# Final norm of an encoder block: three row tiles go through GpSimd and ScalarE, with a root group of their own

## The chip, the cores and the metric

The kernel runs on one NeuronCore of a Trainium2 chip. A core has TensorE (PE), VectorE (DVE), ScalarE (ACT), GpSimd (POOL) and SyncE (SP, which here issues DMAs), an on-chip memory of 128 partitions (SBUF), an accumulator memory that TensorE writes (PSUM), and DMA engines. The metric is the device time of one execution in microseconds, as a median of runs.

## The reference

One block: a mixer of convolutions and projections, a mixture of experts whose output is added to the rows, and a root-mean-square norm of every row at the end. The change touches only what follows the experts:

```
def rmsnorm(x, g):
    y = xf * lax.rsqrt(jnp.mean(xf * xf, axis=-1, keepdims=True) + RMS_EPS)
    return (y * g.astype(jnp.float32)).astype(x.dtype)
...
        x = x + gt2 * hier_moe(h, ...)
    return rmsnorm(x, g_final)
```

There are 1024 rows of 1024 float32 values. `hier_moe` adds, for each row, the outputs of two experts, each scaled by a weight.

## The kernel before

Most of the time is a loop over blocks of 128 (row, expert) pairs: SyncE streams expert weights into SBUF, ScalarE and VectorE split them into a high and a low part, TensorE multiplies, VectorE scales a block's result and GpSimd adds it to the rows `d_x1` in DRAM by an indirect DMA (a scatter). The change lies behind this loop, in the last 40 us.

The rows there are in 8 tiles of 128 rows (tile i is rows 128i to 128i+127, one row on each partition). The rows of the last two expert blocks are handled apart: their results don't go through DRAM, and their rows are called z rows here (`z_x_prev`, `z_x_last`, 128 rows each). Each engine runs its own program in its written order, and semaphores tie them:

- SyncE loads `g_final`, spread over all partitions, into `g_fin`, then the 8 tiles into `f_x` (line 583). Then it waits for tile 0, 1, ... 7 of the output in this order, and stores each (line 586).
- ScalarE takes the sum of squares of each tile and of the two z blocks (`square`, line 1032), and roots of groups of them (`group_root`, line 1041). Groups are ranges of a small table, one column for each of 10 blocks: (0, 2), (2, 5), (5, 10), where columns 8 and 9 are the z blocks.
- VectorE turns sums into mean squares (`mean_square`, line 1632, `f_ms`), and roots into reciprocal roots with a Newton step (`rstd_of`, four short instructions, lines 1638 to 1641). `tile_out` (by `scaled`, line 1645) makes one output tile as `f_x` times `f_rstd` times `g_fin`, in one instruction with two tensors in SBUF. Between them it adds the results of the experts to the z rows: line 1657 for `z_x_prev` (two tensors in SBUF), `y_last` (line 1570: one tensor in PSUM, one in SBUF), and line 1665 for `z_x_last` (PSUM and SBUF). Its last two instructions scale the z rows (`z_o`).
- GpSimd gathers the z rows (line 748), and has nothing to compute after that. At the end it waits until all 8 stores have landed (`f_st`, 16 for each), since a z row overwrites the same row of a stored tile, and then scatters the two z blocks into the output (line 756).

The end of VectorE's program:

```
            tile_out(2, 1)
            tile_out(3, 1)
            dve.wait_ge(y_ev, n_before + 1 + CREDIT_Y)
            dve.wait_ge(s_shared, 1)
            v.tensor_tensor(z_x[1][:], ps[:, 0, :], y_last[:], ALU.add).then_inc(s_z, 1)
            tile_out(4, 1)
            mean_square(2, NT + 2)
            rstd_of(2)
            for i in range(5, NT):
                tile_out(i, 2)
```

Of the kernel before, what the change touches and what calls it, by code (L numbers as in the profile page):

```python
# [29 lines left out]
ALU = mybir.AluOpType  # L30
ACT = mybir.ActivationFunctionType
# [41 lines left out]
def encoder_block(nc, x, c, w_ada, b_ada, g_norm1, w_in, conv_a, w_a_out, conv_b, b_conv_b, ln_g, ln_b,  # L73
                  w_b_out, w_o, g_norm2, w_rg, b_rg, w_re, b_re, w_gate, w_up, w_down, g_final, out):
    S, D = x.shape
    KT = D // P
    NT = S // P
# [13 lines left out]
    with ExitStack() as ctx:  # L91
# [3 lines left out]
        def at(name, offset, shape, dtype):  # L95
            return nc.alloc_sbuf_tensor_at(name, shape, dtype, offset=base + offset)
# [86 lines left out]
        def rt(name, shape, dtype=F32):  # L183
# [65 lines left out]
        f_x = at("f_x", 0, [P, NT, D], F32)  # L249
        y_prev = at("y_prev", (NCH + 4) * 4 * C8, [P, D], F32)  # L250
        y_last = at("y_last", (NCH + 4) * 4 * C8 + T4, [P, D], F32)
        z_x = [at("z_x_prev", oR + GT1 * T4, [P, D], F32), at("z_x_last", oR + A2 * T4, [P, D], F32)]
        f_junk = at("f_junk", (NCH + 2) * 4 * C8, [P, 2, D], F32)
        z_o = at("z_o", (NCH + 3) * 4 * C8, [P, 2, D], F32)
        f_o = [at(f"f_o{i}", o, [P, D], F32) for i, o in enumerate(
            (oX + 4 * T4, oX + 5 * T4, oX + 6 * T4, oX + T4, *((2 * NCH + 2) * 4 * C8 + i * T4 for i in range(4))))]
        g_fin = at("g_fin", oR + SH2 * T4, [P, D], F32)
# [6 lines left out]
        NF = NT + 2  # L264
        f_ss, f_ms, f_root, f_rstd, f_new = (at(n, oM + 2816 + 64 * i, [P, NF], F32)
                                             for i, n in enumerate(("f_ss", "f_ms", "f_root", "f_rstd", "f_new")))
# [16 lines left out]
        def sem(name):  # L283
            return ctx.enter_context(nc.semaphore(name))

        s_par, s_const, s_fill = sem("params_in"), sem("const_ready"), sem("const_steps")
        s_rows_in, s_g2_in, s_wr_in = sem("bias_rows_in"), sem("gfin_in"), sem("router_in")
# [10 lines left out]
        s_ssq, s_rstd, s_xn, s_xT, s_xTev = sem("ssq"), sem("rstd_x"), sem("xn_ready"), sem("xT_ps"), sem("xnT_ready")  # L298
# [5 lines left out]
        s_ln, s_lsig, s_sw, s_bhi, s_blo = sem("ln_t"), sem("ln_sig"), sem("swish"), sem("conf_hi"), sem("conf_lo")  # L304
# [14 lines left out]
        gu_hi, gu_lo, gu_used = sem("gu_hi"), sem("gu_lo"), sem("gu_used")  # L319
# [7 lines left out]
            sem("last_tokens"), sem("same_token"), sem("shared_rows_ps"),  # L327
            sem("z_x_full"))
        s_z, z_out, z_st = sem("z_added"), sem("z_out"), sem("z_stored")
        f_ssq, f_out, f_st = sem("f_ssq"), sem("f_out"), sem("f_stored")  # L330
        a_free, g_free, y_free = sem("short_free"), [sem("gate_a_free"), sem("gate_b_free")], sem("y_free")
        after_wait = sem("after_wait")
        x_full = [sem(f"rows_full{i}") for i in range(NT)]
# [6 lines left out]

        XT_BY_ACT = (3, 5, 6, 7)
        XT_BY_DVE = tuple(i for i in range(NT) if i not in XT_BY_ACT)
        GROUPS = ((0, 2), (2, 5), (5, 10))

        DVE_AT = {}

# [82 lines left out]
        def _(sp):  # L429
# [58 lines left out]
            def load_slab(n):  # L488
                slot, _, before = slab_turn(n)
                sp.wait_ge(w_lo_done, before + 1 + CREDIT_SLAB)  # L490
                sp.dma_start(raw3[:, slot], slab_out(n)).then_inc(wr_full[slot], 16)
# [89 lines left out]
            sp.wait_ge(moe_done, 1)  # L581
            for i in range(NT):
                sp.dma_start(f_x[:, i, :], d_x1[i * P:(i + 1) * P, :]).then_inc(x_full[i], 16)
            for i in range(NT):
                sp.wait_ge(f_out, i + 1)
                sp.dma_start(out[i * P:(i + 1) * P, :], f_o[i][:]).then_inc(f_st, 16)
            sp.wait_ge(f_st, 16 * NT)
            sp.wait_ge(z_st, 32)
# [3 lines left out]
        def _(pool):  # L592
            g = nc.gpsimd
# [122 lines left out]
            n_before = pool.value_load(tab[0:1, NBLK + 1:NBLK + 2], min_val=PAIRS // P - 1, max_val=NBLK - 2)  # L716
# [30 lines left out]
            for n in range(2):  # L747
                g.indirect_dma_start(z_x[n][:], None, d_x1, bass.IndirectOffsetOnAxis(ap=l_idx[:, n:n + 1], axis=0),
                                     bounds_check=S - 1, oob_is_err=False).then_inc(zx_full, 16)


            pool.wait_ge(f_st, 16 * NT)
            pool.wait_ge(s_same, 2)
# [7 lines left out]
        def _(act):  # L761
            a = nc.scalar
# [10 lines left out]
            def square_x(i):  # L773
                act.wait_ge(x_full[i], 16)
                if i >= 2:
                    act.wait_ge(s_ssq, i - 1)
                a.activation(junk0[:, i % 2, :], xn[:, i, :], ACT.Square, accum_out=ss[:, i:i + 1]).then_inc(s_ssq, 1)
# [208 lines left out]
            n_before = act.value_load(tab[0:1, NBLK + 1:NBLK + 2], min_val=PAIRS // P - 1, max_val=NBLK - 2)  # L986
# [41 lines left out]
            def square(n, source):  # L1028

                if n >= 2:  # L1030
                    act.wait_ge(f_ssq, n - 1)
                a.activation(f_junk[:, n % 2, :], source, ACT.Square, accum_out=f_ss[:, n:n + 1]).then_inc(f_ssq, 1)
# [5 lines left out]
            def group_root(p):  # L1038
                gr = slice(*GROUPS[p])
                act.wait_ge(s_msq, 2 * NT + p + 1)  # L1040
                a.activation(f_root[:, gr], f_ms[:, gr], ACT.Sqrt).then_inc(s_root, 1)
# [5 lines left out]
            for i in range(2, 6):  # L1047
                square_x(i)
            group_root(1)
            square_x(6)  # L1050
            square_x(7)
            for n in range(2):
                act.wait_ge(s_z, n + 1)
                square(NT + n, z_x[n][:])
            group_root(2)


        @block.vector
        def _(dve):
# [3 lines left out]
            def step(ins):  # L1063

                steps[0] += 1
                ins.then_inc(dv, 1)
                dve.wait_ge(dv, steps[0])

            def held(s, value):

                dve.wait_ge(s, value)
                dve.sem_inc(after_wait, 1)
# [374 lines left out]
            for i in range(NT):  # L1447
# [23 lines left out]
                scaled = v.scalar_tensor_tensor(hh, xt, rstd[:, i:i + 1], rows[:, A2, :], ALU.mult, ALU.mult)  # L1471
# [45 lines left out]
            for k, first, end in ROW_PARTS:  # L1517
                n = end - first
# [48 lines left out]
            def y_out(dst, blk, used, bank=3):  # L1567

                dve.wait_ge(d_used, used)
                v.scalar_tensor_tensor(dst, ps[:, bank, :], w_all[:, bass.ds(blk, 1)], rows[:, GT2, :], ALU.mult, ALU.mult).then_inc(y_ev, 1)  # L1570
# [10 lines left out]
            n_before = dve.value_load(tab[0:1, NBLK + 1:NBLK + 2], min_val=PAIRS // P - 1, max_val=NBLK - 2)  # L1581
# [47 lines left out]
            def mean_square(p, squares):  # L1629
                gr = slice(*GROUPS[p])  # L1630
                dve.wait_ge(f_ssq, squares)
                v.tensor_scalar(f_ms[:, gr], f_ss[:, gr], 1.0 / D, RMS_EPS, ALU.mult, ALU.add).then_inc(s_msq, 1)

            def rstd_of(p):
                gr = slice(*GROUPS[p])
                dve.wait_ge(s_msq, 2 * NT + p + 1)
                dve.wait_ge(s_root, 2 * NT + p + 1)
                step(v.reciprocal(f_rstd[:, gr], f_root[:, gr]))
                step(v.tensor_tensor(f_new[:, gr], f_rstd[:, gr], f_ms[:, gr], ALU.mult))
                step(v.scalar_tensor_tensor(f_new[:, gr], f_new[:, gr], -0.5, f_rstd[:, gr], ALU.mult, ALU.mult))  # L1640
                v.scalar_tensor_tensor(f_rstd[:, gr], f_new[:, gr], 1.5, f_rstd[:, gr], ALU.add, ALU.mult).then_inc(s_rstd, 1)

            def scaled(dst, source, n, p, done):
                dve.wait_ge(s_rstd, NT + p + 1)
                v.scalar_tensor_tensor(dst, source, f_rstd[:, n:n + 1], g_fin[:], ALU.mult, ALU.mult).then_inc(done, 1)  # L1645

            def tile_out(i, p):
                scaled(f_o[i][:], f_x[:, i, :], i, p, f_out)
# [9 lines left out]
            mean_square(1, 5)  # L1658
            rstd_of(1)
            y_out(y_last[:], n_before, n_before * 2 + 2, 1)  # L1660
            tile_out(2, 1)
            tile_out(3, 1)
            dve.wait_ge(y_ev, n_before + 1 + CREDIT_Y)
            dve.wait_ge(s_shared, 1)
            v.tensor_tensor(z_x[1][:], ps[:, 0, :], y_last[:], ALU.add).then_inc(s_z, 1)
            tile_out(4, 1)
            mean_square(2, NT + 2)
            rstd_of(2)
            for i in range(5, NT):
                tile_out(i, 2)  # L1670
            for n in range(2):
                scaled(z_o[:, n, :], z_x[n][:], NT + n, 2, z_out)


        @block.tensor
        def _(pe):
# [163 lines left out]
            for j in range(KT):  # L1840
                slot, _, _ = slab_turn(n0 + j)
                pe.wait_ge(w_lo_done, n0 + j + 1 + CREDIT_SLAB)
                if j == 1:
                    pe.wait_ge(act_evac, CREDIT_ACT_EVAC + 4 * KT - 1)
                if j >= 2:
                    pe.wait_ge(s_ma, j - 1)
                slab_product(slot, ps[:, j % 2, :], s_alo if j == 0 else None, None,
                             {2: (0, mean_last), 3: (5, variance)}.get(j)).then_inc(pe_slab, 1)
                if j == 1:
                    mean()  # L1850
# [283 lines left out]
```

## Time and profile before

| | |
|---|---|
| median of 3 runs | 1602.11 us (1601.93 to 1602.23) |
| the profiled execution, its own time | 1603.24 us |
| span of its trace, first to last instruction | 1601.6 us |
| PE, DVE, ACT, POOL busy, share of the span | 97%, 83%, 43%, 19% |

The busy shares are means over the whole span and are set by the expert loop. Behind it TensorE has little to do: in the last 20 us it has no instruction. What the end is worth is read from the chain of work that ended last and from the engines' instructions in order of time from about 1562 us on. Times are microseconds from the start of the span; a row of a timeline has the start, the length, the engine, the line, the operation, what is written and read, and its shape.

### The profile page before, as it was taken

How to read it: one execution, taken by the hardware profiler on the slowest of the kernel's cores; microseconds unless marked ns; L12 is line 12 of the kernel's file. 1: busy time of each engine (PE TensorE's matmuls, PEld its weight loads, DVE VectorE, ACT ScalarE, POOL GpSimd, SP SyncE). 2: the span in 40 equal slices, each digit the busy share in tenths (PEclk: the TensorE clock that was granted, in tenths of full speed). 3: DMA queues.
4: the chain of work that ended last, by engine and by line, in shares of the span. 5: the costliest groups of instructions: out<-in, count | busy, mean ns of one | idle time of the engine just before them, and what ended most of it. 6: DMA issues, size and time to landing. Idle time of an engine off the chain costs nothing.

```text
span 1601.6 us, 21226 instructions
## 1 busy us (share of the span) xinstructions
PE 1561.0 (97%) x7106; PEld 1276.8 (80%) x7106; DVE 1325.9 (83%) x1131; ACT 687.2 (43%) x582; POOL 304.8 (19%) x225
## 2 busy tenths in 40 slices
PE   8999999999999999999999999999999999999994
PEld 4788888888888888768888887788888888888882
DVE  5696979797878778789447468999999999999996
ACT  6501111111101010436222126777777777777763
POOL 2000000000101010000001003354344334433441
PEclk9999999999999999999999999999999999999997
DMA  9242333232324141644453347999999999999976
GB/s 359 93 119 79 107 102 108 76 118 65 118 65 129 54 144 46 217 150 140 158 181 138 118 176 271 385 373 398 390 366 369 383 377 389 374 390 385 378 275 239
DMA packets 167951, 352.61 MB, mean 220 GB/s; under 512 B 17479, under 2 KB 91239, under 8 KB 167907
## 3 DMA queue, kind: packets, MB, share of 16 engines
q1 hardware_dynamic: 150836, 309.57, 53.0%
q0 software_dynamic: 16992, 42.32, 8.7%
q8 instruction: 25, 0.41, 0.1%
q10 hardware_dynamic: 81, 0.17, 0.0%
q14 instruction: 17, 0.14, 0.0%
HBM read 324.90 MB, written 46.67 MB: 232 GB/s over the span
## 4 chain that ended last, share of the span: by engine, by line
PE 88%; DVE 6%; DMA 3%; issue 2%; ACT 1%; SPq 0%; DVEq 0%; POOLq 0%; POOL 0%; ACTq 0%
PE ps L1681 28%; PE ps L1683 28%; PE ps L1682 28%; PE ps L2008 2%; DMA xn<-in_x_dram 1%; DVE conv_acc_b L1253 1%; PE ps L2013 1%; DMA w_raw<-in_w_in_dram 1%; DVE e_lo L1545 1%; PE ps L1902 1%; DMA stream<-d_short 1%; DVE f_o L1645 0%; DVE e_lo L1549 0%; PE ps L1886 0%; DMA e_raw<-in_w_down_dram 0%
## 5 line engine op out<-in xcount | busy, mean ns | idle before, releaser
L1681 PE MATMUL ps<-A_hi,w_hi 128*128 128x512 f32 x1024 | 399.8, 390 | 6.0 <-DVE w_lo L1092 4.1
L1683 PE MATMUL ps<-A_hi,w_lo 128*128 128x512 f32 x1024 | 398.6, 389 | 0.0
L1682 PE MATMUL ps<-A_lo,w_hi 128*128 128x512 f32 x1024 | 398.5, 389 | 0.0
L1545 DVE TENSOR_TENSOR e_lo<-e_raw,e_hi 128x2048 fp32r<-128x2048 f32 x132 | 301.1, 2289 | 10.4 <-ACT e_hi L958 10.3
L1253 DVE SCALAR_TENSOR_TENSOR conv_acc_b<-glu,colc,conv_acc_b 128x1024 f32<-128x1024 f32 x232 | 298.0, 1285 | 10.2 <-DVE rows L1238 0.6
L958 ACT CAST e_hi<-e_raw 128x2048 fp32r<-128x2048 f32 x132 | 252.2, 1913 | 44.0 <-PE ps L1683 43.8
L1681 PEld LDWEIGHTS ps<-A_hi,w_hi 128*128 128x128 f32 x1024 | 192.3, 188 | 49.3 <-DVE w_lo L1092 5.4
L1682 PEld LDWEIGHTS ps<-A_lo,w_hi 128*128 128x128 f32 x1024 | 192.2, 188 | 40.2 <-issue 0.5
L1683 PEld LDWEIGHTS ps<-A_hi,w_lo 128*128 128x128 f32 x1024 | 192.2, 188 | 40.0
L1681 PE MATMUL ps<-e_hi,xT_hi 128*128 128x512 f32 x528 | 212.5, 403 | 1.7 <-DVE xT_lo L1553 1.7
L1683 PE MATMUL ps<-e_hi,xT_lo 128*128 128x512 f32 x528 | 207.1, 392 | 0.0
L1682 PE MATMUL ps<-e_lo,xT_hi 128*128 128x512 f32 x528 | 206.4, 391 | 0.0
L1549 DVE TENSOR_TENSOR e_lo<-e_raw,e_hi 128x2048 fp32r<-128x2048 f32 x64 | 146.0, 2283 | 0.0
L697 POOL DMA_INDIRECT d_x<-y_sb,s_idx x31 | 85.9, 2772 | 305.3 <-DVE y_sb L1570 276.7
L812 ACT CAST w_hi<-w_raw 128x1024 fp32r<-128x1024 f32 x72 | 73.6, 1047 | 156.1 <-PE ps L1683 153.1
L964 ACT CAST e_hi<-e_raw 128x2048 fp32r<-128x2048 f32 x64 | 122.3, 1913 | 42.1 <-PE ps L1683 42.1
L1092 DVE TENSOR_TENSOR w_lo<-w_raw,w_hi 128x1024 fp32r<-128x1024 f32 x72 | 88.0, 1223 | 61.0 <-ACT w_hi L812 57.8
L1683 PEld LDWEIGHTS ps<-e_hi,xT_lo 128*128 128x128 f32 x528 | 99.5, 188 | 21.7
L1681 PEld LDWEIGHTS ps<-e_hi,xT_hi 128*128 128x128 f32 x528 | 99.9, 189 | 20.5 <-DVE xT_lo L1553 1.8
L1682 PEld LDWEIGHTS ps<-e_lo,xT_hi 128*128 128x128 f32 x528 | 99.9, 189 | 18.9
L1681 PE MATMUL ps<-e_hi,hT_hi 128*128 128x512 f32 x264 | 104.7, 397 | 3.0 <-DVE hT_lo L1564 3.0
L1683 PE MATMUL ps<-e_hi,hT_lo 128*128 128x512 f32 x264 | 104.2, 395 | 0.0
(329 smaller groups left out, 2001.1 us busy)
## 6 DMA issues: line engine op xcount, KB each, us to landing
e_raw<-in_w_gate_dram SPq DMA_DIRECT2D x132, 512.0 KB
e_raw<-in_w_up_dram SPq DMA_DIRECT2D x132, 512.0 KB
e_raw<-in_w_down_dram SPq DMA_DIRECT2D x66, 1024.0 KB, 7.8
w_raw<-in_w_in_dram SPq DMA_DIRECT2D x56, 512.0 KB, 4.3
stream<-in_w_ada_dram SPq DMA_DIRECT2D x36, 512.0 KB, 5.8
xn<-in_x_dram SPq DMA_DIRECT2D x8, 512.0 KB, 11.3
ada_a<-in_w_ada_dram SPq DMA_DIRECT2D x8, 512.0 KB, 10.4
d_short<-conv_acc_a POOLq DMA_DIRECT2D x8, 512.0 KB, 4.1
```

The costliest lines, as they stand in the source:

```text
L697: g.indirect_dma_start(d_x1, bass.IndirectOffsetOnAxis(ap=idx_ap, axis=0), rows_ap, None, bounds_check=S - 1, oob_is_err=False, compute_op ...
L812: a.copy(w_hi[:, slot, :], w_raw[:, slot, :]).then_inc(w_hi_done, 1)
L958: a.copy(e_hi[:, q, :], e_raw[:, q, :]).then_inc(gu_hi, 1)
L964: a.copy(e_hi[:, 4 + q, :], e_raw[:, 4 + q, :]).then_inc(d_hi, 1)
L1092: v.tensor_tensor(w_lo[:, slot, :], w_raw[:, slot, :], w_hi[:, slot, :].bitcast(F32), ALU.subtract).then_inc(w_lo_done, 1)
L1253: lstep(v.scalar_tensor_tensor(conv_acc_b[:], glu[:, t:t + S], w, conv_acc_b[:], ALU.mult, ALU.add))
L1545: v.tensor_tensor(e_lo[:, q, :], e_raw[:, q, :], e_hi[:, q, :].bitcast(F32), ALU.subtract).then_inc(gu_lo, 1)
L1549: v.tensor_tensor(e_lo[:, 4 + q, :], e_raw[:, 4 + q, :], e_hi[:, 4 + q, :].bitcast(F32), ALU.subtract).then_inc(d_lo, 1)
L1681: t.matmul(dst, st_hi, mv_hi, start=first, stop=False)
L1682: t.matmul(dst, st_hi, mv_lo, start=False, stop=False)
L1683: return t.matmul(dst, st_lo, mv_hi, start=False, stop=last)
L2008: last = t.transpose(ps[:, bank, k * P:(k + 1) * P], cols_k, ident[:])
```

## The change

- GpSimd multiplies tiles 4, 5 and 6 of `f_x` by `g_fin` into the output buffers `f_o`, as soon as a tile is loaded. This needs no root. The instruction reads two tensors in SBUF.
- ScalarE then scales these three in place by `f_rstd` (`tile_by_act`): tiles 4 and 5 before the square of the second z block, tile 6 as its last instruction.
- The groups of roots are (0, 2), (2, 5), (5, 8), (8, 10): tiles 5 to 7 have one of their own and no longer wait for the z blocks.
- VectorE makes tiles 0 to 3 and 7 only; its order around them is changed.
- SyncE stores in the order 0, 1, 2, 4, 5, 3, 6, 7.
- `f_gain` and `f_act` are semaphores of an earlier stage used again; both stand at 8 (`KT`) by then.

```
+        f_gain, f_act, GAIN0 = s_bhi, s_sw, KT
...
-        GROUPS = ((0, 2), (2, 5), (5, 10))
+        GROUPS = ((0, 2), (2, 5), (5, NT), (NT, NF))
+        BY_GAIN = (4, 5, 6)
...
-            for i in range(NT):
-                sp.wait_ge(f_out, i + 1)
+            n_dve, n_act = 0, GAIN0
+            for i in (0, 1, 2, 4, 5, 3, 6, 7):
+                if i in BY_GAIN:
+                    n_act += 1
+                    sp.wait_ge(f_act, n_act)
+                else:
+                    n_dve += 1
+                    sp.wait_ge(f_out, n_dve)
                 sp.dma_start(out[i * P:(i + 1) * P, :], f_o[i][:]).then_inc(f_st, 16)
...
+            pool.wait_ge(s_g2_in, 16)
+            held(gu_used, n_before * 4 + 4)
+            for i in BY_GAIN:
+                pool.wait_ge(x_full[i], 48)
+                g.tensor_tensor(f_o[i][:], f_x[:, i, :], g_fin[:], ALU.mult).then_inc(f_gain, 1)
 
             pool.wait_ge(f_st, 16 * NT)
...
+            def tile_by_act(n, p):
+                i = BY_GAIN[n]
+                act.wait_ge(f_gain, GAIN0 + n + 1)
+                act.wait_ge(s_rstd, NT + p + 1)
+                a.activation(f_o[i][:], f_o[i][:], ACT.Copy, scale=f_rstd[:, i:i + 1]).then_inc(f_act, 1)
+
             square_x(6)
             square_x(7)
-            for n in range(2):
-                act.wait_ge(s_z, n + 1)
-                square(NT + n, z_x[n][:])
+            act.wait_ge(s_z, 1)
+            square(NT, z_x[0][:])
             group_root(2)
+            tile_by_act(0, 1)
+            tile_by_act(1, 2)
+            act.wait_ge(s_z, 2)
+            square(NT + 1, z_x[1][:])
+            group_root(3)
+            tile_by_act(2, 2)
...
             y_out(y_last[:], n_before, n_before * 2 + 2, 1)
+            mean_square(2, NT)
             tile_out(2, 1)
-            tile_out(3, 1)
+            rstd_of(2)
             dve.wait_ge(y_ev, n_before + 1 + CREDIT_Y)
             dve.wait_ge(s_shared, 1)
             v.tensor_tensor(z_x[1][:], ps[:, 0, :], y_last[:], ALU.add).then_inc(s_z, 1)
-            tile_out(4, 1)
-            mean_square(2, NT + 2)
-            rstd_of(2)
-            for i in range(5, NT):
-                tile_out(i, 2)
+            tile_out(3, 1)
+            mean_square(3, NF)
+            tile_out(7, 2)
+            rstd_of(3)
             for n in range(2):
-                scaled(z_o[:, n, :], z_x[n][:], NT + n, 2, z_out)
+                scaled(z_o[:, n, :], z_x[n][:], NT + n, 3, z_out)
```

VectorE's program before, from `y_last` on. `f_o_170` is output tile 0, `f_o_177` tile 7; the shape is partitions x elements, so `f_ms` 128x5 is a group of five blocks:

```order
L1570 SCALAR_TENSOR_TENSOR y_last<-ps,w_all,rows 128x1024
L1645 SCALAR_TENSOR_TENSOR f_o_172<-f_x,f_rstd,g_fin 128x1024
L1645 SCALAR_TENSOR_TENSOR f_o_173<-f_x,f_rstd,g_fin 128x1024
L1663 REGISTER_ALU
L1665 TENSOR_TENSOR z_x_last<-ps,y_last 128x1024
L1645 SCALAR_TENSOR_TENSOR f_o_174<-f_x,f_rstd,g_fin 128x1024
L1632 TENSOR_SCALAR f_ms<-f_ss 128x5
L1638 RECIPROCAL f_rstd<-f_root 128x5
L1639 TENSOR_TENSOR f_new<-f_rstd,f_ms 128x5
L1640 SCALAR_TENSOR_TENSOR f_new<-f_new,f_rstd 128x5
L1641 SCALAR_TENSOR_TENSOR f_rstd<-f_new,f_rstd 128x5
L1645 SCALAR_TENSOR_TENSOR f_o_175<-f_x,f_rstd,g_fin 128x1024
```

The same place in the changed program (its lines are numbered 24 or 25 higher here):

```order
L1594 SCALAR_TENSOR_TENSOR y_last<-ps,w_all,rows 128x1024
L1656 TENSOR_SCALAR f_ms<-f_ss 128x3
L1669 SCALAR_TENSOR_TENSOR f_o_172<-f_x,f_rstd,g_fin 128x1024
L1662 RECIPROCAL f_rstd<-f_root 128x3
L1663 TENSOR_TENSOR f_new<-f_rstd,f_ms 128x3
L1664 SCALAR_TENSOR_TENSOR f_new<-f_new,f_rstd 128x3
L1665 SCALAR_TENSOR_TENSOR f_rstd<-f_new,f_rstd 128x3
L1688 REGISTER_ALU
L1690 TENSOR_TENSOR z_x_last<-ps,y_last 128x1024
L1669 SCALAR_TENSOR_TENSOR f_o_173<-f_x,f_rstd,g_fin 128x1024
L1656 TENSOR_SCALAR f_ms<-f_ss 128x2
L1669 SCALAR_TENSOR_TENSOR f_o_177<-f_x,f_rstd,g_fin 128x1024
```

Tile 3 moved behind the add into `z_x_last`, the root group of tiles 5 to 7 moved ahead of that add, and tiles 4 to 6 are gone from this engine.

GpSimd's program in the changed kernel, from the gathers of the z rows to its end; of these rows the program before has all but the three of line 763 and the waiting row ahead of them:

```order
L756 DMA z_x_prev<-d_x,l_idx 128x1024
L756 DMA z_x_last<-d_x,l_idx 128x1024
L612 REGISTER_ALU
L763 TENSOR_TENSOR f_o_174<-f_x,g_fin 128x1024
L763 TENSOR_TENSOR f_o_175<-f_x,g_fin 128x1024
L763 TENSOR_TENSOR f_o_176<-f_x,g_fin 128x1024
L769 DMA out_dram<-z_o,z_idx 1024x1024
L769 DMA out_dram<-z_o,l_idx 1024x1024
```

The three products stand between the gathers and the final scatters, where GpSimd only waited before.

## Rows read from the trace of the kernel before

**Rows 1.** Chain of work that ended last, 1586 to 1603: start, length, what
```profile
1587.84 2.85 DMA out_dram<-f_o
...
1591.52 1.01 POOL out_dram L756
```

**Rows 2.** Timeline of DVE, 1571.9 to 1590: start, length, line, operation, out<-in, shape
```profile
1571.95 2.48 DVE L1645 SCALAR_TENSOR_TENSOR f_o<-f_x,f_rstd,g_fin 128x1024 f32<-128x1024 f32 x2
1574.35 1.22 DVE L1657 TENSOR_TENSOR z_x_prev<-z_x_prev,y_prev 128x1024 f32<-128x1024 f32 x1
1575.49 0.17 DVE L1632 TENSOR_SCALAR f_ms<-f_ss 128x3 f32<-128x3 f32 x1
1575.99 0.18 DVE L1638 RECIPROCAL f_rstd<-f_root 128x3 f32<-128x3 f32 x1 [0.34 <-ACT f_root L1041]
...
1576.78 1.28 DVE L1570 SCALAR_TENSOR_TENSOR y_last<-ps,w_all,rows 128x1024 f32<-128x1024 f32 x1
1577.98 2.47 DVE L1645 SCALAR_TENSOR_TENSOR f_o<-f_x,f_rstd,g_fin 128x1024 f32<-128x1024 f32 x2
1580.37 1.22 DVE L1665 TENSOR_TENSOR z_x_last<-ps,y_last 128x1024 f32<-128x1024 f32 x1
1581.50 1.27 DVE L1645 SCALAR_TENSOR_TENSOR f_o<-f_x,f_rstd,g_fin 128x1024 f32<-128x1024 f32 x1
...
1584.13 3.68 DVE L1645 SCALAR_TENSOR_TENSOR f_o<-f_x,f_rstd,g_fin 128x1024 f32<-128x1024 f32 x3
```

**Rows 3.** Timeline of ACT, 1575 to 1584
```profile
1575.69 0.21 ACT L1041 ACTIVATE f_root<-f_ms 128x3 f32<-128x3 f32 x1 [0.27 <-DVE f_ms L1632]
...
1577.88 1.04 ACT L1032 ACTIVATE f_junk<-z_x_prev 128x1024 f32<-128x1024 f32 x1
...
1581.62 1.06 ACT L1032 ACTIVATE f_junk<-z_x_last 128x1024 f32<-128x1024 f32 x1 [2.61 <-DVE z_x_last L1665]
```

**Rows 4.** Line 795, ScalarE scaling a tile in place: ns min/median/max
```profile
L795 ACT ACTIVATE xn<-xn,rstd x8: 1131/1132/1147, 9.7 to 29.9; 128x1024 f32<-128x1024 f32 x8
```

**Rows 5.** Line 640, GpSimd adding two tensors of one tile's size: ns min/median/max
```profile
L640 POOL TENSOR_TENSOR conf<-conf x7: 2402/2411/2413, 132.7 to 589.7; 128x1024 f32<-128x1024 f32 x7
```

**Rows 6.** Line 1211, a copy of 41 columns on VectorE: ns min/median/max
```profile
L1211 DVE COPY colc<-cols x8: 178/2104/2416, 58.9 to 589.7; 128x41 f32 x6, 128x41 f32<-128x41 f32 x2
```

**Rows 7.** Timeline of both engines, 208 to 212.5
```profile
208.90 2.40 POOL L640 TENSOR_TENSOR conf<-conf 128x1024 f32<-128x1024 f32 x1 [9.40 <-DVE conf L1257]
...
209.32 2.03 DVE L1211 COPY colc<-cols 128x41 f32 x1 [0.70 <-DVE conf L1257]
```

**Rows 8.** Timeline of GpSimd and VectorE, 600 to 606
```profile
601.18 1.23 DVE L1092 TENSOR_TENSOR w_lo<-w_raw,w_hi 128x1024 fp32r<-128x1024 f32 x1
601.22 2.10 POOL L643 COPY conf_sum<-conf 128x1024 f32<-128x1024 f32 x1 [9.11 <-DVE glu L1215]
602.33 1.53 DVE L1251 TENSOR_SCALAR conv_acc_b<-glu,colc 128x1024 f32<-128x1024 f32 x1
```

**Rows 9.** Line 1251 on VectorE: ns min/median/max
```profile
L1251 DVE TENSOR_SCALAR conv_acc_b<-glu,colc x8: 807/808/1530, 70.2 to 602.3; 128x1024 f32<-128x1024 f32 x8
```

**Rows 10.** Timelines of GpSimd, then VectorE, 1542 to 1548
```profile
1543.85 1.30 POOL L726 COPY s_idx<-idx_all 128x1 int32 x1
...
1542.81 4.58 DVE L1545 TENSOR_TENSOR e_lo<-e_raw,e_hi 128x2048 fp32r<-128x2048 f32 x2 [0.30 <-ACT e_hi L958]
```

**Rows 11.** Line 726, GpSimd's copy of one column: ns min/median/max
```profile
L726 POOL COPY s_idx<-idx_all x30: 203/1305/1397, 1028.0 to 1543.8; 128x1 int32 x30
```

**Rows 12.** Line 583, the load of tile 4 (issued 1564.3), and its landing
```profile
L583 SPq DMA_DIRECT2D f_x<-d_x x1: 553/553/553, 1564.3 to 1564.3; - x1
...
DMA to landing us min/median/max: 8.7/8.7/8.7
```

**Rows 13.** Line 586, the store of tile 4 (issued 1582.8), to its landing
```profile
DMA to landing us min/median/max: 2.6/2.6/2.6
```

**Rows 14.** A stretch with only stores: engines' busy time, clock, DMA share, GB/s
```profile
1588.00:1590.00 2.00, 0.00 (x0) 0.00 (x0) 2.00 (x2) 0.00 (x0) 0.00 (x0) 0.50 1.02 412
```

## The prediction

> **What bounds the kernel now.** I read the chain that ended last first, from its end backwards. The last scatters wait for one thing: the store of tile 7 lands at 1590.69 (issued 1587.84, 2.85 us) [rows 1]. GpSimd begins the first scatter 0.8 us later, and the rest of the run, 10.9 us of scatters and closing, hangs on that landing. So the question is when the eighth store lands. Ahead of it is VectorE: from 1571.95 to 1590 it is hardly idle. Its row order [rows 2] shows what an early finish would need: tiles 0 and 1, the add into `z_x_prev`, a root group, `y_last`, tiles 2 and 3, the add into `z_x_last`, tile 4, a root group that waits for the square of `z_x_last` (ScalarE starts it at 1581.62 [rows 3]), and then tiles 5 to 7, 1.2 us each. The change takes three tiles off this chain and gives them to GpSimd and ScalarE, which are idle for most of the stretch. The stores are close to a second limit: where only stores run, the DMA engines are busy the whole time at 412 GB/s [rows 14], so a tile of 0.524 MB takes 1.27 to 1.29 us, against 1.2 us in which VectorE makes one. A store alone lands 2.6 us after its issue [rows 13], taken as 2.66 from 1582.78 to 1585.44.
>
> **The change as written, with GpSimd costing the others nothing.** Up to `y_last` (1576.78 to 1578.06) nothing of VectorE moves. Then the short `f_ms` (0.17), tile 2 until 1579.45. ScalarE ends the square of `z_x_prev` at about 1579.0 (1577.88 plus 1.04 and a short read of the sum), takes the root by 1579.25, and VectorE's four short instructions (0.79, from 1575.99 to the start of `y_last` at 1576.78 in the group before [rows 2]) end at 1580.3. The add into `z_x_last` then starts at about 1580.3, as before (1580.37): a root group stands where tile 3 stood. Tile 3 ends at 1582.8, `f_ms` 1582.97, tile 7 at 1584.2. ScalarE scales in 1.13 us a tile [rows 4]: tile 4 from 1579.25, tile 5 from 1580.4, then the square at 1581.62 as before, root, and tile 6 from 1583.25 to 1584.4. Six stores then follow one another, tile 2 issued 1579.5 and landed 1582.2; five more at 1.29 give 1588.6. That is 2.1 us ahead of 1590.69. The z rows are ready at 1587.5, ahead of it too. So three tiles off VectorE (3.6 us) bring 2.1 at most: the DMA engines limit the rest, and they do so with or without the order of the roots.
>
> **What the three products cost VectorE.** No row of before shows GpSimd multiplying beside VectorE's `tile_out`. Three sets of rows bound it.
> - GpSimd's own time: its add of two SBUF tensors of this size takes 2.40 to 2.41 us, seven times [rows 5].
> - A VectorE instruction that starts in that time waits for its end. A copy of 41 columns takes 0.178 us alone and 2.10 as a median [rows 6]; the one at 209.32 ends at 211.35, and GpSimd's add at 211.30 [rows 7]. Likewise at 602.33: 1.53 instead of 0.81 us [rows 8, 9], while GpSimd copies.
> - A VectorE instruction with two SBUF tensors holds GpSimd in turn, and GpSimd gets in between two that follow without a gap. The one-column copy (0.20 alone, 1.31 as a median of 30 [rows 11]) starts at 1543.85 inside a 2.29 us subtraction and ends at 1545.15, just behind the seam of two of them at 1545.10 [rows 10]. The copy at 601.22 waits for `w_lo` to end at 602.4, takes 0.9 us, and the next VectorE instruction pays [rows 8].
>
> So both engines use something that one of them has at a time, for whole instructions, and a seam is enough for the other to get it. `tile_out` (`f_x`, `g_fin`) and the add into `z_x_prev` have two SBUF tensors, as the subtraction has, so I take them as excluded by a product too. The lower bound of a product's cost is 0, the upper one 2.41 us; I take 2.33, from the start of the hold to its end, since rows 7 are nearest in form (same GpSimd operands) and show a full wait.
>
> The Trainium skill, page "SBUF — State Buffer", section "Who interferes with whom", states the same for just this pair: a VectorE instruction with two SBUF inputs contends with a GpSimd instruction that reads SBUF, and whoever comes second blocks until the first is done. By that rule the case below holds; if rows 6 and 7 told only of copies, the sum would be that of the part above.
>
> **The sum.** Tile 4 of `f_x` lands at 1564.3 + 8.7 = 1573.0 [rows 12], tiles 5 and 6 a transfer of 1.3 us each later; the GpSimd gathers are long done and `g_fin` is there. At 1573.0 VectorE is in tile 0 or at the seam to tile 1.
> - Product 4 takes the seam behind tile 1, 1574.4 to 1576.7. The add into `z_x_prev` is held until 1576.7, and ends 1577.9.
> - Product 5 takes 1577.9 to 1580.2. Under it lie `f_ms`, the root and the reciprocal (0.7 us), which have one SBUF input; the Newton product has two and waits until 1580.2.
> - Product 6 gets in between the short instructions, 1580.3 to 1582.6, and the group is done at 1582.9 to 1583.1 instead of 1576.8: 7.0 us of holds, less 0.7 that lay beside other work, is 6.2.
> - From there GpSimd is quiet. `y_last` to 1584.2, tile 2 to 1585.5, short group to 1586.3, add to 1587.4, tile 3 to 1588.6, tile 7 to 1590.0; ScalarE makes tile 6 by 1590.2. Tile 2's store lands at 1588.2, five more by 1.29: 1594.65. Against 1590.69 that is +3.96. Seams that no longer overlap (three times 0.05 to 0.1) make it +4.1.
>
> If product 4 wins the seam before tile 1 instead, everything up to the group shifts by one instruction and the group's end is the same. Who waits for VectorE here is ScalarE (the squares of tiles 6 and 7 queue behind the root of group 1) and the stores; TensorE has nothing to do after the add into `z_x_last` has its input. The span becomes 1605.7, the profiled execution 1607.3; the median lay 1.13 below the profiled execution (1602.11 against 1603.24), so the difference is put on the median: 1606.2.
>
> **The rivals.**
> 1. *No exclusion* (the other side). `tile_out` and the adds run beside the products at their old length. The time is then 1602.11 - 2.1 = 1600.0. For it: no row shows a float product of two SBUF tensors on VectorE held. Against: rows 6 to 11. It decides by the first product: above 0.65 us of cost on the chain per product the gain is gone.
> 2. *Product 6 falls beside `y_last`.* `y_last` reads PSUM and one SBUF tensor, so it can run beside a product. If the short group wins its seams, `y_last` runs 1580.7 to 1581.9, product 6 1580.8 to 1583.1, and tile 2 waits until then: its store lands 1587.0, the last 1593.4, +2.7, 1604.8. For it: GpSimd needs some time from an instruction's start until it takes the slot. Against: the group has three seams in 0.6 us.
> 3. *`f_ms` is held as well.* With product 4 at the seam before tile 1, product 6 begins just as the add into `z_x_prev` ends, `f_ms` waits until 1582.5, the root and the squares of tiles 6 and 7 behind it end at about 1585.3, and the next `f_ms` waits for them behind `y_last`: +5.0, 1607.1. The copies of rows 6 were held with one input, which speaks for it. The Trainium skill, page "VectorE: DVE Perf Modes", section "Mode 2×_2P — use both read ports for one tensor", says why such an instruction could be: one with a single SBUF source may use both read ports. The trace agrees for the copy in rows 6.
> 4. *Something milder.* Both engines slow each other but none waits a whole instruction: 0 to +2, 1603.
>
> That the change doesn't do what it says (a product late, so that ScalarE waits for it) costs nothing here: by 1582.6 all three are done, and in the case without exclusion by 1580.4, when tile 5 is wanted at 1580.4.
>
> **How the numbers follow.** Forecast 1606.2 with a chance of 0.48; rival 1 0.14, rival 2 0.17, rival 3 0.15, rival 4 0.06. The range leaves out rival 1 and a little at either end: 1602.8 to 1608.0; the upper end is all three products at 2.41 us on the path (+7.2 - 2.1 = +5.1), with room for late squares. A difference of 0.2% is 3.2 us, about what a measurement can tell from none. Over 1605.3 lie nearly all of the forecast's case (0.43 of 0.48), rival 3 and a little of rival 2: slower 0.60. Under 1598.9 only a rival 1 with the stores not queueing: 0.03. Within: 0.37.
>
> **What would show it.** `z_x_prev`'s add, or tile 1 at the latest, with a length near 3.5 us instead of 1.2; a short Newton instruction of about 2.3 us; three GpSimd products with recorded lengths of 2.4 to 3.6 us, each ending where a VectorE instruction begins to move. The last store lands near 1594.7, at steps of 1.29 us from tile 2 on. Tiles of 1.28 us on VectorE beside the products would prove the exclusion wrong, and the last store would land near 1588.6. Rival 2 shows as a long tile 2, rival 3 as a long `f_ms`.

## The result

| | before | after |
|---|---|---|
| median | 1602.17 us (1601.13 to 1603.47, 8 runs) | 1607.01 us (1605.01 to 1608.42, 8 runs) |
| ratio, 95% interval | | 1.0024 (1.0015 to 1.0033) |
| the profiled execution, its time and span | 1603.24, 1601.6 us | 1608.04, 1606.4 us |

The kernel became slower: 0.24% of 1602 us is 3.9 us by the ratio, and the raw medians lie 4.8 apart. In the profiled execution of the changed kernel the stretch in question also begins 1.11 us later (tile 0 at 1573.06, before at 1571.95 [rows 2]), which the change need not explain: in the profiled executions of the experiments below, tile 0 begins anywhere from 1569.93 to 1574.26. So the traces are compared from the start of tile 0 to the landing of the last store: 18.74 us before (1571.95 to 1590.69 [rows 1, 2]), 22.42 after. That is +3.7. This is one execution of each kernel; the ratio above rests on 8.

The chain that ended last, after (start, length, what); it answers to [rows 1]:

```profile
1575.54 3.35 DVE z_x_prev L1681
1578.89 2.24 DVE f_ms L1656
...
1581.67 1.76 DVE f_new L1663
...
1591.29 4.19 DMA out_dram<-f_o
```

The last store lands at 1595.48. Three instructions of VectorE stand in this chain with lengths that [rows 2] don't have. Its timeline shows them in their places, to be set against [rows 2]:

```profile
1573.06 2.48 DVE L1669 SCALAR_TENSOR_TENSOR f_o<-f_x,f_rstd,g_fin 128x1024 f32<-128x1024 f32 x2
1575.45 3.44 DVE L1681 TENSOR_TENSOR z_x_prev<-z_x_prev,y_prev 128x1024 f32<-128x1024 f32 x1
1578.81 2.30 DVE L1656 TENSOR_SCALAR f_ms<-f_ss 128x3 f32<-128x3 f32 x1
1581.46 0.18 DVE L1662 RECIPROCAL f_rstd<-f_root 128x3 f32<-128x3 f32 x1 [0.34 <-ACT f_root L1054]
1581.67 1.75 DVE L1663 TENSOR_TENSOR f_new<-f_rstd,f_ms 128x3 f32<-128x3 f32 x1
...
1583.78 1.28 DVE L1594 SCALAR_TENSOR_TENSOR y_last<-ps,w_all,rows 128x1024 f32<-128x1024 f32 x1
```

And GpSimd's timeline, where the three products are one row:

```profile
1574.71 8.69 POOL L763 TENSOR_TENSOR f_o<-f_x,g_fin 128x1024 f32<-128x1024 f32 x3 [6.29 <-DMA f_x<-d_x]
```

One row doesn't show where the second and third product begin; that is read from the held instructions. The products end at 1583.40 and the held `f_new` at 1583.42. The add is 2.22 us longer than its 1.22, `f_ms` 2.13 longer than 0.17, the Newton product 1.59 longer than 0.16: 5.9 us together. `y_last`, which began 4.83 us after tile 0, now begins 10.72 after it. What the change saves behind that point, 2.2 us, is what is left between 5.9 and 3.7.

### The profile page after: what moved, and what is told of

It reads as the page before. It is cut to its first block, busy times and chain, and to the rows that moved or that the text cites. A ratio compares the mean times of both kernels' runs of the same rounds, so it can differ in the third digit from the quotient of the medians.

```text
span 1606.4 us, 21241 instructions
## 1 busy us (share of the span) xinstructions
PE 1561.0 (97%) x7106; PEld 1277.4 (80%) x7106; DVE 1328.6 (83%) x1133; ACT 690.6 (43%) x586; POOL 312.3 (19%) x228
## 4 chain that ended last, share of the span: by engine, by line
PE 88%; DVE 6%; DMA 3%; issue 1%; ACT 1%; SPq 0%; POOLq 0%; ACTq 0%; DVEq 0%; POOL 0%
PE ps L1705 28%; PE ps L1707 28%; PE ps L1706 28%; PE ps L2032 2%; DMA xn<-in_x_dram 1%; DVE conv_acc_b L1277 1%; PE ps L2037 1%; DMA w_raw<-in_w_in_dram 1%; DVE e_lo L1569 1%; PE ps L1926 1%; DMA stream<-d_short 1%; DVE e_lo L1573 0%; PE ps L1910 0%; DMA e_raw<-in_w_down_dram 0%; PE ps L1834 0%
```

## The experiments

The theory is that of the prediction: an instruction of VectorE with two SBUF tensors and a product on GpSimd exclude each other for whole instructions, and this is the whole loss. The rivals are that any work of GpSimd at that place costs, that a product has a fixed price, or that the new order of roots and tiles costs. Each kernel below was timed beside the kernel before on the same chip, the four experiments from "GpSimd writes only" to "groups and order alone" on one chip and the last three on another. The medians of before were 1603.07 us there and 1602.88 us here (1602.17 for the changed kernel), so the differences below are the ratio less one, times 1603. "From tile 0" is the time from the start of tile 0 to the landing of the last store in the one trace of each kernel, less the 18.74 of before. "Later" means that the products wait for root groups.

| kernel | median, us | ratio (95%) | difference, us | from tile 0, us |
|---|---|---|---|---|
| the changed kernel | 1607.01 | 1.0024 (1.0015 to 1.0033) | +3.9 | +3.7 |
| GpSimd writes only | 1601.13 | 0.9987 (0.9978 to 0.9996) | -2.1 | -1.8 |
| products of half width | 1603.43 | 1.0005 (0.9996 to 1.0014) | +0.8 | +0.4 |
| before, with the products added | 1607.95 | 1.0036 (1.0022 to 1.0050) | +5.8 | +6.4 |
| groups and order alone | 1603.12 | 1.0002 (0.9993 to 1.0011) | +0.3 | +0.2 |
| g_final in PSUM, products later | 1600.85 | 0.9987 (0.9979 to 0.9996) | -2.1 | -2.0 |
| g_final in PSUM alone | 1605.44 | 1.0017 (1.0008 to 1.0026) | +2.7 | +2.9 |
| products later alone | 1604.47 | 1.0014 (1.0003 to 1.0025) | +2.2 | +2.0 |

### GpSimd writes, but does not read

```
-                g.tensor_tensor(f_o[i][:], f_x[:, i, :], g_fin[:], ALU.mult).then_inc(f_gain, 1)
+                g.iota(f_o[i][:], pattern=[[1, D]], base=1, channel_multiplier=0,
+                       allow_small_or_imprecise_dtypes=True).then_inc(f_gain, 1)
```

> The changed kernel, but GpSimd fills tiles 4 to 6 of the output buffer with a ramp (it writes 1024 columns and reads no SBUF) in place of its product of two SBUF tensors; those three tiles lack x and g_final. Theory (VectorE instructions with two SBUF inputs wait for a GpSimd instruction that reads SBUF): the add into z_x_prev takes 1.2 us again, the first Newton product 0.17, the last store lands 2.1 us before that of the kernel before, 1600.0 us. Rival A (any GpSimd instruction at that place holds VectorE, writes included): three holds stay, 1606 or more. Rival B (only instructions that use both read and both write ports of VectorE are held, as the short f_ms may be): f_ms is long, 1601 to 1603.

Measured: -2.1 us. GpSimd and VectorE in this kernel, in order of time:

```profile
1571.95 0.99 POOL L763 IOTA f_o<- 128x1024 f32 x1 [4.99 <-DMA f_x<-d_x]
1573.32 0.99 POOL L763 IOTA f_o<- 128x1024 f32 x1 [0.38 <-DMA f_x<-d_x]
1574.53 0.99 POOL L763 IOTA f_o<- 128x1024 f32 x1 [0.21 <-DMA f_x<-d_x]
```

```profile
1571.48 2.48 DVE L1670 SCALAR_TENSOR_TENSOR f_o<-f_x,f_rstd,g_fin 128x1024 f32<-128x1024 f32 x2
1573.87 1.22 DVE L1682 TENSOR_TENSOR z_x_prev<-z_x_prev,y_prev 128x1024 f32<-128x1024 f32 x1
1575.01 0.53 DVE L1657 TENSOR_SCALAR f_ms<-f_ss 128x3 f32<-128x3 f32 x1
```

The first filling lies wholly inside the two tiles, whose 2.48 us are those of [rows 2], and the second overlaps tile 1 and the add, which keeps its 1.22. So GpSimd's writes hold no instruction with two SBUF tensors. A filling is shorter than a product, 0.99 us, but here it lengthens them by nothing at all. Rival A falls. Rival B is seen in small: `f_ms`, with one SBUF source, takes 0.53 instead of 0.17 and ends at 1575.54, as the third filling does at 1575.52. That took 0.36 us on VectorE. The run also shows what the rest of the change is worth where the products cost next to nothing: 2.1 us (0.6 to 3.5 by the interval), 1.8 in the trace.

### Products of half the width

```
+            for i in BY_GAIN:
+                g.memset(f_o[i][:, D // 2:], 1.0)
...
-                g.tensor_tensor(f_o[i][:], f_x[:, i, :], g_fin[:], ALU.mult).then_inc(f_gain, 1)
+                g.tensor_tensor(f_o[i][:, 0:D // 2], f_x[:, i, 0:D // 2], g_fin[:, 0:D // 2], ALU.mult).then_inc(f_gain, 1)
```

> The changed kernel with GpSimd's three products on 512 of 1024 columns; the other half is filled with ones before the rows land, so half of tiles 4 to 6 lacks x and g_final. Theory (holds as long as the product): holds of about 1.15 instead of 2.2 us, three of them, so some 3.3 us come back: 1602.7 us (0.5 above before). Rival (a fixed cost for each product, whatever its length): 1606 to 1607.

Measured: +0.8 (0 lies in its interval), 3.1 us under the changed kernel. The same three instructions are held:

```profile
1572.47 2.18 DVE L1683 TENSOR_TENSOR z_x_prev<-z_x_prev,y_prev 128x1024 f32<-128x1024 f32 x1
1574.58 1.23 DVE L1658 TENSOR_SCALAR f_ms<-f_ss 128x3 f32<-128x3 f32 x1
...
1576.35 0.67 DVE L1665 TENSOR_TENSOR f_new<-f_rstd,f_ms 128x3 f32<-128x3 f32 x1
```

The added times are 0.96, 1.06 and 0.50 against 2.22, 2.13 and 1.59 with whole products: they fall by 1.1 to 1.3 us each, about half a product, as was expected. A fixed price falls.

### The kernel before, with the products added

The three products run as in the change; VectorE overwrites their tiles, and the old order, groups and stores stay.

```
+            pool.wait_ge(s_g2_in, 16)
+            held(gu_used, n_before * 4 + 4)
+            for i in (4, 5, 6):
+                pool.wait_ge(x_full[i], 48)
+                g.tensor_tensor(f_o[i][:], f_x[:, i, :], g_fin[:], ALU.mult).then_inc(f_gain, 1)
...
+            dve.wait_ge(f_gain, GAIN0 + 3)
             tile_out(4, 1)
```

> The kernel before, with GpSimd's three products added as in the change but not used: VectorE writes tiles 4 to 6 over them, and waits for them before tile 4. Theory: the products cost VectorE the same three holds in its old order, less what is hidden: 5.9 us, 1608.0 us. Rival (the loss comes from the new order and the new root group, not from the products): 1602 to 1603.

Measured: +5.8. Here the first product is recorded 0.71 us behind the start of tile 0, in the changed kernel 1.65, and it won the other seam (the moment between two instructions of VectorE), ahead of tile 1:

```profile
1570.96 9.41 POOL L756 TENSOR_TENSOR f_o<-f_x,g_fin 128x1024 f32<-128x1024 f32 x3 [5.33 <-DMA f_x<-d_x]
```

```profile
1570.25 4.63 DVE L1651 SCALAR_TENSOR_TENSOR f_o<-f_x,f_rstd,g_fin 128x1024 f32<-128x1024 f32 x2
1574.81 3.37 DVE L1663 TENSOR_TENSOR z_x_prev<-z_x_prev,y_prev 128x1024 f32<-128x1024 f32 x1
1578.10 2.30 DVE L1638 TENSOR_SCALAR f_ms<-f_ss 128x3 f32<-128x3 f32 x1
...
1580.95 0.16 DVE L1645 TENSOR_TENSOR f_new<-f_rstd,f_ms 128x3 f32<-128x3 f32 x1
```

Two tiles take 4.63 instead of 2.48: an output tile itself is held, by 2.15. The Newton product is free, since the three holds have been paid before it: 2.15, 2.15 and 2.13 us, 6.4 together, which is also the loss from tile 0. The products alone account for more than the whole loss of the change (3.7), as they must if its other half gains.

### Groups and order alone

VectorE makes all eight tiles in the order of the change, GpSimd and ScalarE none:

```
-                g.tensor_tensor(f_o[i][:], f_x[:, i, :], g_fin[:], ALU.mult).then_inc(f_gain, 1)
...
             tile_out(3, 1)
+            tile_out(4, 1)
             mean_square(3, NF)
-            tile_out(7, 2)
+            for i in range(5, NT):
+                tile_out(i, 2)
             rstd_of(3)
```

> The changed kernel without GpSimd's products and without ScalarE's tiles: VectorE makes all eight tiles, with the root groups and the early order of the change (root of tiles 5 to 7 ahead of the add into z_x_last, tile 7 ahead of the last root group). Theory: the wait for the last root goes (0.3 us), stores are bound by the DMA engines: -0.3, 1601.8 us. Rival (the reordering itself is what costs): 1604 or more.

Measured: +0.3, within the interval of no change. The order costs nothing that can be measured, so the rival falls, but the 0.3 us hoped for aren't there either. The trace says where they are (VectorE, then ScalarE):

```profile
1577.68 0.17 DVE L1648 TENSOR_SCALAR f_ms<-f_ss 128x3 f32<-128x3 f32 x1 [0.32 <-ACT f_junk L1040]
```

```profile
1572.75 1.06 ACT L1040 ACTIVATE f_junk<-f_x 128x1024 f32<-128x1024 f32 x1 [0.55 <-DMA f_x<-d_x]
```

Behind `y_last`, VectorE now waits 0.32 us for ScalarE's square of tile 7, the last of the group. Taking that group early turns a wait for the root into one for its squares. The size of this wait is that of one execution: ScalarE had itself waited 0.55 us for the load of tile 4, which it doesn't in the trace before, and so all later squares came late.

### g_final in PSUM, and products where VectorE needs no second SBUF tensor

If the theory holds, the loss can be avoided with the same products. VectorE's output tiles get `g_final` from PSUM, where ScalarE copies it while it waits for the first root, and so have one SBUF tensor. The matmuls for `z_x_last` move to another part of PSUM for it. GpSimd's products (tiles 3, 5, 6; the stores go 0, 1, 2, 3, 5, 4, 6, 7) each wait for a root group, so that they start with two long instructions of that kind ahead of them.

```
+            act.wait_ge(s_g2_in, 16)
+            act.wait_ge(hd, n_before + 1 + CREDIT_HID)
+            a.copy(ps[:, 0, :], g_fin[:]).then_inc(g_ps, 1)
             group_root(0)
...
-                v.scalar_tensor_tensor(dst, source, f_rstd[:, n:n + 1], g_fin[:], ALU.mult, ALU.mult).then_inc(done, 1)
+                v.scalar_tensor_tensor(dst, source, f_rstd[:, n:n + 1], ps[:, 0, :], ALU.mult, ALU.mult).then_inc(done, 1)
...
-        BY_GAIN = (4, 5, 6)
+        BY_GAIN = (3, 5, 6)
...
+                pool.wait_ge(s_rstd, NT + 1 + n)
...
-            mean_square(2, NT)
             tile_out(2, 1)
+            mean_square(2, NT)
             rstd_of(2)
```

> The full computation. g_final lies in PSUM for VectorE (ScalarE copies it there while it waits for the first root; the shared product of the z rows moves to another part of PSUM), so each output tile and z_o have one SBUF tensor. GpSimd's three products (tiles 3, 5, 6; VectorE makes 4 in place of 3) wait for the root groups 0, 1 and 2, so that they begin as VectorE starts two long instructions of that kind; the f_ms of group 2 comes behind tile 2. Theory (only a second SBUF tensor is held, and the three holds are the whole loss): no long instruction on VectorE is held, the last store lands about 2.1 us before that of the kernel before, 1600.0 us, faster than both. Rival (GpSimd's reads slow VectorE whatever its sources): tiles and y_last beside the products take 1.28 plus the overlap, 1604 to 1607.

Measured: -2.1 (0.6 to 3.4 by the interval), as expected. It computes the whole reference and is faster than both kernels. Its products, then its VectorE:

```profile
1573.52 2.41 POOL L765 TENSOR_TENSOR f_o<-f_x,g_fin 128x1024 f32<-128x1024 f32 x1 [4.64 <-DMA f_x<-d_x]
1578.66 2.38 POOL L765 TENSOR_TENSOR f_o<-f_x,g_fin 128x1024 f32<-128x1024 f32 x1 [2.73 <-DVE f_rstd L1670]
1582.31 2.37 POOL L765 TENSOR_TENSOR f_o<-f_x,g_fin 128x1024 f32<-128x1024 f32 x1 [1.27 <-DVE f_rstd L1670]
```

```profile
1573.48 2.47 DVE L1674 SCALAR_TENSOR_TENSOR f_o<-f_x,f_rstd,ps 128x1024 f32<-128x1024 f32 x2
...
1578.47 1.28 DVE L1599 SCALAR_TENSOR_TENSOR y_last<-ps,w_all,rows 128x1024 f32<-128x1024 f32 x1
1579.67 1.27 DVE L1674 SCALAR_TENSOR_TENSOR f_o<-f_x,f_rstd,ps 128x1024 f32<-128x1024 f32 x1
1580.86 0.21 DVE L1661 TENSOR_SCALAR f_ms<-f_ss 128x3 f32<-128x3 f32 x1
...
1582.17 1.22 DVE L1695 TENSOR_TENSOR z_x_last<-ps,y_last 128x1024 f32<-128x1024 f32 x1
```

Every product takes 2.37 to 2.41, its time alone [rows 5], and every VectorE instruction beside one its usual 1.2 to 1.3. Both engines read SBUF during the products; what is gone is VectorE's second SBUF tensor, and the short instructions lie outside the products, but for an `f_ms` at the end of the second and of the third. The first of these is 0.04 longer. The rival that GpSimd's reads slow VectorE whatever its sources falls.

### Each half of that kernel alone

Against the kernel with both, this one has `g_final` in PSUM, but neither the waits nor the moved `f_ms`, and the tiles and stores of the change:

```
-        BY_GAIN = (3, 5, 6)
+        BY_GAIN = (4, 5, 6)
...
-                pool.wait_ge(s_rstd, NT + 1 + n)
```

> The changed kernel with g_final in PSUM for VectorE and nothing else: products of tiles 4 to 6 start as the rows land. Theory: product 4 runs beside tile 1 instead of behind it, holds the add into z_x_prev for 1 us instead of 2.2; f_ms and the Newton product are held as before. The last store is 1.2 us earlier than in the changed kernel: +2.7 against before, 1604.8 us. Rival (tile_out's second SBUF tensor is the cause of the loss): 1600 to 1601.

```profile
1572.73 8.01 POOL L764 TENSOR_TENSOR f_o<-f_x,g_fin 128x1024 f32<-128x1024 f32 x3 [6.18 <-DMA f_x<-d_x]
```

```profile
1571.15 2.47 DVE L1673 SCALAR_TENSOR_TENSOR f_o<-f_x,f_rstd,ps 128x1024 f32<-128x1024 f32 x2
1573.54 2.68 DVE L1685 TENSOR_TENSOR z_x_prev<-z_x_prev,y_prev 128x1024 f32<-128x1024 f32 x1
1576.14 2.31 DVE L1660 TENSOR_SCALAR f_ms<-f_ss 128x3 f32<-128x3 f32 x1
...
1579.00 1.75 DVE L1667 TENSOR_TENSOR f_new<-f_rstd,f_ms 128x3 f32<-128x3 f32 x1
```

Measured: +2.7, as expected; in the trace the last store is 0.75 us earlier than in the changed kernel, where 1.2 was expected. Product 4 starts at 1572.73 beside tile 1, which isn't held, and leaves 1.46 us of hold for the add (1.0 was expected). The other two holds are untouched.

The waits, tiles and order without PSUM, again against the kernel with both:

```
-                v.scalar_tensor_tensor(dst, source, f_rstd[:, n:n + 1], ps[:, 0, :], ALU.mult, ALU.mult).then_inc(done, 1)
+                v.scalar_tensor_tensor(dst, source, f_rstd[:, n:n + 1], g_fin[:], ALU.mult, ALU.mult).then_inc(done, 1)
```

> The waits, tiles and order of the run with PSUM, but g_final in SBUF for VectorE. Theory: product 3 holds tile 1 for 2.2 us, product 5 runs beside y_last and holds tile 2 for the remaining 1.2 us, product 6 beside the add into z_x_last and holds tile 4 for 1.2 us: in all about +1.5 against before, 1603.6 us. Rival (the order of the products doesn't matter, three whole holds stay): 1606 to 1607.

```profile
1581.47 2.35 POOL L764 TENSOR_TENSOR f_o<-f_x,g_fin 128x1024 f32<-128x1024 f32 x1 [4.75 <-DVE f_rstd L1666]
1586.23 2.36 POOL L764 TENSOR_TENSOR f_o<-f_x,g_fin 128x1024 f32<-128x1024 f32 x1 [2.41 <-DVE f_rstd L1666]
```

```profile
1574.26 4.74 DVE L1670 SCALAR_TENSOR_TENSOR f_o<-f_x,f_rstd,g_fin 128x1024 f32<-128x1024 f32 x2
...
1582.48 2.43 DVE L1670 SCALAR_TENSOR_TENSOR f_o<-f_x,f_rstd,g_fin 128x1024 f32<-128x1024 f32 x1
...
1587.23 2.44 DVE L1670 SCALAR_TENSOR_TENSOR f_o<-f_x,f_rstd,g_fin 128x1024 f32<-128x1024 f32 x1
```

Measured: +2.2, where 1.5 was expected (1.5 lies in the interval). The holds are those that were named: 2.26 us on one of the first two tiles, then 1.16 and 1.17 on one tile each, where the product's first half lay beside `y_last` and the add into `z_x_last`. The sum of the holds is 4.6, and 4.6 less the 2.1 gained is 2.5, against 2.2 measured and 2.0 in the trace. The expectation named the same holds and came to 1.5, so it took 1.0 us of them as hidden, and doesn't say behind what; that much isn't. Neither half alone gains, both together do: without PSUM the tiles are held, without the waits the short instructions and the add are.

## Why the prediction was right

The forecast was 1606.2, and +4.1 as a difference; measured are 1607.0 and +3.9 by the ratio (2.4 to 5.3 by its interval; the raw medians lie 4.8 apart). The mechanism was right. One step in its working was wrong, and the number stood in spite of it.

- **What bounds it.** The last store sets the end, before and after. After, it landed at 1595.48, and the first scatter began at 1596.31, the same 0.83 us later.
- **The change at no cost, 2.1 us gained.** Borne out twice, as far as the intervals tell: -2.1 with GpSimd writing only (-1.8 in the trace), and -2.1 with three products kept but next to nothing held (-2.0 in the trace; it has other tiles and another order). The rest of the argument, that 3.6 us less on VectorE bring no more because six stores follow at the rate of [rows 14], fits as well: with GpSimd writing only, tile 2 is done at 1579.25, and 2.66 and five times 1.29 later is 1588.36, where the last store landed at 1588.41; from 1581 to 1588 the DMA engines were busy the whole time there, at 396 GB/s.
- **The exclusion.** Right: the add is held by 2.22 in the changed kernel, an output tile by 2.15 and 2.26 in two of the experiments, and with GpSimd writing only neither is held. The size taken, 2.33 us from a recorded length of 2.41, was 0.1 to 0.2 too large: a full hold measures 2.13 to 2.26, less than the recorded length.
- **Product 4 behind tile 1, the add held.** As forecast: it is recorded from 1574.71 on, inside tile 1, and the add ends 3.35 us behind tile 1.
- **What product 5 and 6 met.** Here a step was wrong. The prediction let `f_ms`, root and reciprocal run under product 5 (0.7 us hidden) and product 6 slip in between the short instructions. In the trace `f_ms` is held by product 5 for 2.13 us, which was the mechanism of rival 3, without the late squares that rival 3 built on it. Product 6 then lies beside root and reciprocal, and the Newton product waits for the rest, 1.59. The hidden part, 0.5 us, is nearly the same, so the sum stood: the holds are 5.9 where the prediction had 6.2 (its own terms, 7.0 less 0.7, give 6.3), and group 1 is done at 1583.82, which is 10.76 behind tile 0, against 1582.9 to 1583.1, or 10.95 to 11.15 behind it. That this step did no harm is partly luck: `f_ms` and the Newton product follow one another on the same chain, so it hardly mattered which of them a product met.
- **Stores.** Last landing forecast 22.7 us behind tile 0's start (1594.65), measured 22.42. From the start of `y_last` on it is 11.65 forecast (from the group's end at 1583.0) and 11.70 measured.
- **Rivals.** Rival 1 and rival 4 are out by the traces. Rival 2 (product 6 beside `y_last`) didn't come about: by then product 6 was over. What it relied on, that `y_last` can run beside a product, is true (1.28 us in the PSUM kernel).
- **What the pages said.** The Trainium skill, page "SBUF — State Buffer", section "Who interferes with whom", has a VectorE instruction with two SBUF inputs contend with a GpSimd instruction that reads SBUF, and not with one that only writes it. Both halves agree with the traces here: 2.2 us for the add behind a product that reads, nothing for it behind a filling that only writes. The Trainium skill, page "VectorE: DVE Perf Modes", section "Mode 2×_2P — use both read ports for one tensor", by which one with a single SBUF source may use both read ports, had been kept for rival 3 alone. `f_ms` of 3 columns, 2.30 us instead of 0.17, fits it, so it should have stood in the main case; no run here tells this reason from another for the hold of `f_ms`.

What stays open: why `f_ms` is held and the reciprocal isn't, and whether another choice or order of tiles would bring more than 2.1 us; only two were run with GpSimd's products in use.

## What to carry to other kernels

Before work goes from VectorE to an idle GpSimd, look at what VectorE does in that time: here an instruction of it with two SBUF tensors that met a product waited until the product was done, and three products of 2.4 us cost 5.9 us on a chain where three tiles of 1.2 were to be saved. The price isn't in the mean busy share of either engine, but the trace before shows it, in instructions whose length is that of someone else's [rows 6, 7]. With the second operand in PSUM, and each product started with long instructions of that kind ahead, three products of the same size cost next to nothing (2.1 us gained instead of 3.9 lost); either measure alone didn't do it (+2.7, +2.2).

## What the runs showed of the hardware that was not expected

- The short `f_ms` of 3 columns has one SBUF source and is held all the same, behind a product (2.30 us) and even behind a filling that only writes (0.53 instead of 0.17). The reciprocal of 3 columns beside product 6 keeps its 0.18, so it isn't every short instruction. Which property decides wasn't tested.
- GpSimd's ramp over 1024 float32 columns takes 0.99 us, against 2.4 us for a product of two tensors.
- A product recorded as 2.37 to 2.42 us where it has a row of its own holds a VectorE instruction that waits for all of it for 2.13 to 2.26.
